# Triangular systems by block doubling: second products and subtraction over the changed columns alone, with constant matmuls ahead of them

## What is computed

```python
m = jnp.where(strict, jnp.einsum('nbhik,nbhjk->nbhij', k_beta, kc) * decay, 0.0)
a = jnp.eye(C, dtype=f32) + m
u = lax.linalg.triangular_solve(a, v_beta, left_side=True, lower=True, unit_diagonal=True)
w = lax.linalg.triangular_solve(a, k_beta * jnp.exp(gcum)[..., None],
                                left_side=True, lower=True, unit_diagonal=True)
```

## Time and profile before

| what | value |
|---|---|
| median of 3 executions | 2620.18 us (2619.04 to 2622.69) |
| the profiled execution | 2623.88 us, its span 2622.1 us |
| PE busy | 2503.3 us, 95% of the span |
| DVE busy | 1726.1 us, 66% |
| ACT busy, POOL busy | 1216.9 us, 657.5 us |
| stage of the triangular systems | 597.1 to 724.9 us of the span |

### The profile page before, as it was taken

One profiled execution on the slowest core, in us unless ns is written; L12 is line 12 of the kernel. 1 busy time (PEld: TensorE's weight loads), 2 busy tenths in 40 slices (PEclk: granted clock), 3 DMA queues, 4 the chain that ended last, 5 costly groups with the idle time before them and its releaser, 6 DMA issues.

```text
span 2622.1 us, 42984 instructions
## 1 busy us (share of the span) xinstructions
PE 2503.3 (95%) x16456; PEld 2171.4 (83%) x16456; DVE 1726.1 (66%) x3444; ACT 1216.9 (46%) x2307; POOL 657.5 (25%) x594
## 2 busy tenths in 40 slices
PE   8999999997879999999999999999999999999998
PEld 6777887886767877888888887789999889989998
DVE  4787487898776677356764456676663576746766
ACT  4322324751153523324433325656555568555684
POOL 0111112003213201112111122121135543655435
PEclk9999999998889999999999999999999999999999
DMA  7554452220002455333453442237544444444444
GB/s 285 170 183 161 144 177 81 81 89 2 2 1 72 162 181 173 136 132 125 157 177 133 156 145 76 97 105 249 190 158 151 138 153 140 167 145 145 154 137 145
DMA packets 119324, 359.05 MB, mean 137 GB/s; under 512 B 13136, under 2 KB 15312, under 8 KB 118736
## 3 DMA queue, kind: packets, MB, share of 16 engines
q1 hardware_dynamic: 119120, 356.30, 39.8%
HBM read 355.20 MB, written 1.05 MB: 136 GB/s over the span
## 4 chain that ended last, share of the span: by engine, by line
PE 72%; DVE 12%; ACT 6%; issue 4%; DMA 4%; POOL 2%; DVEq 0%; SPq 0%; POOLq 0%; ACTq 0%
PE ps L1954 20%; PE ps L1957 20%; PE ps L1955 19%; DMA ring<-w_stream 4%; ACT spl L2303 2%; DVE work L2573 2%; DVE big L2573 2%; DVE spl L2549 1%; PE ps L2018 1%; DVE big L2767 1%; PE ps L2211 1%; PE ps L1979 1%; PE ps L1981 1%; PE ps L1980 1%; PE ps L2248 1%
## 5 line engine op out<-in xcount | busy, mean ns | idle before, releaser
L1954 PE MATMUL ps<-bigr,spl 128*128 128x256 f32 (+1 forms) x3846 | 1307.4, 340 | 31.4 <-DVE spl L2549 24.3
L1957 PE MATMUL ps<-bigr,spl 128*128 128x256 f32 (+1 forms) x3846 | 1287.7, 335 | 3.5 <-POOL bigr L3030 3.2
L1955 PE MATMUL ps<-bigr,spl 128*128 128x256 f32 (+1 forms) x3846 | 1285.2, 334 | 0.0
L2549 DVE TENSOR_TENSOR spl<-ring,spl 128x512 fp32r<-128x512 f32 x838 | 657.9, 792 | 581.3 <-ACT spl L2303 578.1
L2303 ACT ACTIVATE spl<-ring 128x512 fp32r<-128x512 f32 x1024 | 629.9, 628 | 746.2 <-PE ps L1957 503.8
L1954 PEld LDWEIGHTS ps<-bigr,spl 128*128 128x128 f32 x3846 | 730.3, 190 | 129.9 <-DVE spl L2549 32.2
L1957 PEld LDWEIGHTS ps<-bigr,spl 128*128 128x128 f32 x3846 | 730.2, 190 | 84.1 <-POOL bigr L3030 10.3
L1955 PEld LDWEIGHTS ps<-bigr,spl 128*128 128x128 f32 x3846 | 730.8, 190 | 72.9 <-issue 1.7
L3030 POOL TENSOR_TENSOR bigr<-work,bigr 128x512 fp32r<-128x512 f32 (+1 forms) x192 | 198.5, 1037 | 925.0 <-ACT bigr L2307 924.9
L3025 POOL TENSOR_TENSOR spl<-ring,spl 128x512 fp32r<-128x512 f32 x186 | 253.8, 1365 | 275.0 <-ACT spl L2303 274.3
L2307 ACT ACTIVATE bigr<-work 128x512 fp32r<-128x512 f32 (+1 forms) x224 | 117.3, 526 | 259.8 <-DVE work L2633 163.0
(11 more groups left out here) (312 smaller groups left out, 2389.7 us busy)
## 6 DMA issues: line engine op xcount, KB each, us to landing
ring<-w_stream SPq DMA_DIRECT2D x512, 512.0 KB, 3.4
big<-w_stream SPq DMA_DIRECT2D x280, 256.0 KB, 3.1
big<-w_stream SPq DMA_DIRECT2D x16, 512.0 KB, 10.1
X<-x_t SPq DMA_DIRECT2D x2, 1024.0 KB, 15.4
cst<-consts SPq DMA_DIRECT2D x1, 1537.5 KB, 9.0
X<-mem_t SPq DMA_DIRECT2D x1, 1024.0 KB, 5.8
out_t<-X SPq DMA_DIRECT2D x8, 128.0 KB, 2.1
prm<-params SPq DMA_DIRECT2D x1, 252.5 KB, 2.7
```

Of the source, the lines that this page charges most:

```text
L1954: pe.matmul(out, hi, x[0], start=k == 0, stop=False)
L1955: pe.matmul(out, lo, x[0], start=False, stop=False)
L1957: finish(pe.matmul(out, hi, x[1], start=False, stop=k == nk - 1), tile, key if k == nk - 1 else None)
L2549: dve.tensor_tensor(lo_half(h), raw_half(h), hi_half(h), SUB).then_inc(*sig("lo", h, by="lo_dve"))
```

## The change

The tiles T and U of direction 1 change places (U comes first), and some of the tiles move to other columns, so that the changed columns of T and of U are one access pattern. `block_half` picks every second block of lv columns. The second products have 32 moving columns in place of 64 and write 32 columns each, packed, so that both products of a system fill 256 columns of the bank (128 at level 32). The subtraction goes over these alone. For direction 0, `level_u` on TensorE issues two matmuls on constants into the same bank, before it waits for the mask; the second products overwrite their result. The weights of all products stay 64x64 and their number stays as it was.

```diff
-        lane = [[(B(LN0 + d * 1024, 256), B(LN0 + d * 1024 + 256, 512), accQ[:, 0:256] if d else B(LN0 + 768, 256)) for d in range(2)],
-                [(w_[:, 0:256], arow[:, 512 * d:512 * d + 512], w_[:, 256:512]) for d, w_ in enumerate((w_mean, w_rstd))]]
+        def lane_of(d, whole, at, Mt, Pm):
+            first, second = whole[:, at:at + 256], whole[:, at + 256:at + 512]
+            T_, U_ = (second, first) if d else (first, second)
+            return Mt, T_, U_, Pm, whole[:, at:at + 576]
+
+        lane = [[lane_of(d, B(0, WK), LN0 + (1024 if d else 256), B(LN0 + (1536 if d else 0), 256), accQ[:, 0:256] if d else B(LN0 + 768, 256)) for d in range(2)],
+                [lane_of(0, arow, 0, w_rstd[:, 0:256], w_rstd[:, 256:512]),
+                 lane_of(1, work, 7 * 512, arow[:, 512:768], arow[:, 768:1024])]]
+
+        def block_half(ap, lv, x):
+            return ap.rearrange("p (n s i) -> p n s i", s=2, i=lv)[:, :, x, :]
+
+        def changed(d, lv, TU):
+
+            if lv == 32:
+                return block_half(TU[:, 0:256] if d else TU[:, 256:512], lv, 1 - d)
+            both = TU[:, 0:512 + 2 * lv].rearrange("p (u m) -> p u m", u=2)[:, :, 0:256]
+            return both.rearrange("p u (n s i) -> p u n s i", s=2, i=lv)[:, :, :, 0, :]
...
             def warm(n, bank, free):
                 w.all(free, done)
+                constants(bank, n)
+
+            def constants(bank, n):
                 w.wait_ge(*done("cond"))
                 moving = csr[:, 0:256].rearrange("p (o n) -> p o n", o=1).broadcast_to([128, 2, 256])
                 for _ in range(n):
...
             def level_u(h, d, lv, b, free):
-                _, TU, Pm = lane[h % 2][d]
-                w.all(free, done)
+                _, T_, U_, Pm, _ = lane[h % 2][d]
+                w.all(free, done)
+                if not d:
+                    constants(b, 2)
                 w.wait_ge(*done("lvp", h, d, lv))
+                to_t, to_u = (b[:, 128:256], b[:, 0:128]) if d or lv == 32 else (b[:, 0:128], b[:, 128:256])
                 for c in range(8):
                     p, t, rows = chunk(c)
                     cs_ = slice(t * 64, t * 64 + 64)
-                    us_ = slice(256 + t * 64, 256 + t * 64 + 64)
+                    at = slice(t * 32, t * 32 + 32)
                     if lv < 32:
-                        pe.matmul(b[rows, cs_], TU[rows, us_], Pm[rows, cs_], start=True, stop=True)
-                    ins = pe.matmul(b[rows, us_], Pm[rows, cs_], TU[rows, us_], start=True, stop=True)
+                        pe.matmul(to_t[rows, at], U_[rows, cs_], block_half(Pm[rows, cs_], lv, d), start=True, stop=True)
+                    ins = pe.matmul(to_u[rows, at], Pm[rows, cs_], block_half(U_[rows, cs_], lv, 1 - d), start=True, stop=True)
                 ins.then_inc(*sig("lvb", h, d, lv))
...
             def level_u(h, d, lv, b, free):
-                TU = lane[h % 2][d][1]
-                a = 0 if lv < 32 else 256
+                x = changed(d, lv, lane[h % 2][d][4])
+                if lv < 32:
+                    y = b[:, 0:256].rearrange("p (u n i) -> p u n i", u=2, i=lv)
+                else:
+                    y = b[:, 0:128].rearrange("p (n i) -> p n i", i=lv)
                 w.wait_ge(*done("lvb", h, d, lv))
-                dve.tensor_tensor(TU[:, a:512], TU[:, a:512], b[:, a:512], SUB).then_inc(*sig("tu", h, d, lv))
+                dve.tensor_tensor(x, x, y, SUB).then_inc(*sig("tu", h, d, lv))
```

More of the change, by code:

```diff
@@ L2092, in unit_turn @@
             def unit_turn(h, d, b, free):
-                U = lane[h % 2][d][1][:, 256:512]
+                U = lane[h % 2][d][2]
                 w.all(free, done)
@@ L2114, in level_p @@
             def level_p(h, d, lv, b, free):
-                Mt, TU, _ = lane[h % 2][d]
+                Mt, T_ = lane[h % 2][d][0:2]
                 w.all(free, done)
@@ L2121, in level_p @@
                     cs_ = slice(t * 64, t * 64 + 64)
-                    ins = pe.matmul(b[rows, cs_], Mt[rows, cs_], TU[rows, cs_], start=True, stop=True)
+                    ins = pe.matmul(b[rows, cs_], Mt[rows, cs_], T_[rows, cs_], start=True, stop=True)
                 ins.then_inc(*sig("lva", h, d, lv))
             def level_u(h, d, lv, b, free):
-                _, TU, Pm = lane[h % 2][d]
+                _, T_, U_, Pm, _ = lane[h % 2][d]
                 w.all(free, done)
+                if not d:
+                    constants(b, 2)
                 w.wait_ge(*done("lvp", h, d, lv))
+                to_t, to_u = (b[:, 128:256], b[:, 0:128]) if d or lv == 32 else (b[:, 0:128], b[:, 128:256])
                 for c in range(8):
@@ L2131, in level_u @@
                     cs_ = slice(t * 64, t * 64 + 64)
-                    us_ = slice(256 + t * 64, 256 + t * 64 + 64)
+                    at = slice(t * 32, t * 32 + 32)
                     if lv < 32:
-                        pe.matmul(b[rows, cs_], TU[rows, us_], Pm[rows, cs_], start=True, stop=True)
-                    ins = pe.matmul(b[rows, us_], Pm[rows, cs_], TU[rows, us_], start=True, stop=True)
+                        pe.matmul(to_t[rows, at], U_[rows, cs_], block_half(Pm[rows, cs_], lv, d), start=True, stop=True)
+                    ins = pe.matmul(to_u[rows, at], Pm[rows, cs_], block_half(U_[rows, cs_], lv, 1 - d), start=True, stop=True)
                 ins.then_inc(*sig("lvb", h, d, lv))
             def u_values(h, d, b, free):
-                Ub = lane[h % 2][d][1][:, 0:256]
+                Ub = lane[h % 2][d][1]
                 w.all(free, done)
@@ L2149, in w_keys @@
             def w_keys(h, d, bb, free):
-                Uw = lane[h % 2][d][2]
+                Uw = lane[h % 2][d][3]
                 w.all(free, done)
@@ L2412, in decay @@
             def decay(h, d, b, taken):
-                E = lane[h % 2][d][2]
+                E = lane[h % 2][d][3]
                 w.wait_ge(*done("de_min", h, d))
@@ L2418, in unit_turn @@
                 w.wait_ge(*done("ut", h, d))
-                act.activation(lane[h % 2][d][1][:, 0:256], b[:, 0:256], ACTF.Copy).then_inc(*sig("utc", h, d))
+                act.activation(lane[h % 2][d][1], b[:, 0:256], ACTF.Copy).then_inc(*sig("utc", h, d))
             def q_decay(h, d, b, free, e, efree):
@@ L2779, in decay @@
             def decay(h, d, b, taken):
-                Mt, _, E = lane[h % 2][d]
+                Mt, _, _, E, _ = lane[h % 2][d]
                 w.wait_ge(*done("grow", h, d))
@@ L2800, in level_p @@
             def level_p(h, d, lv, b, free):
-                Pm = lane[h % 2][d][2]
+                Pm = lane[h % 2][d][3]
                 w.wait_ge(*done("lva", h, d, lv))
@@ L2807, in level_u @@
             def level_u(h, d, lv, b, free):
-                TU = lane[h % 2][d][1]
-                a = 0 if lv < 32 else 256
+                x = changed(d, lv, lane[h % 2][d][4])
[3 more added lines that the diff above has]
+                    y = b[:, 0:128].rearrange("p (n i) -> p n i", i=lv)
                 w.wait_ge(*done("lvb", h, d, lv))
-                dve.tensor_tensor(TU[:, a:512], TU[:, a:512], b[:, a:512], SUB).then_inc(*sig("tu", h, d, lv))
+                dve.tensor_tensor(x, x, y, SUB).then_inc(*sig("tu", h, d, lv))
             def scale_u(h, d):
-                _, TU, Pm = lane[h % 2][d]
-                U = TU[:, 256:512]
+                _, T_, U, Pm, _ = lane[h % 2][d]
                 w.wait_ge(*done("tu", h, d, 32))
-                dve.tensor_tensor(four(TU[:, 0:256]), four(U), cA4[:, :, 2 + d, h:h + 1].broadcast_to([128, 4, 64]), MUL).then_inc(*sig("ub", h, d))
+                dve.tensor_tensor(four(T_), four(U), cA4[:, :, 2 + d, h:h + 1].broadcast_to([128, 4, 64]), MUL).then_inc(*sig("ub", h, d))
                 w.wait_ge(*done("cb"))
@@ L3056, in unit @@
             def unit(h, d, bG):
-                Mt, TU, _ = lane[h % 2][d]
-                U = TU[:, 256:512]
+                Mt, _, U = lane[h % 2][d][0:3]
                 w.wait_ge(*done("mm", h, d))
```

## The result

The changed kernel takes 2625.63 us in the median of 13 runs (2621.06 to 2632.17), the kernel before 2621.25 in the median of as many (2614.92 to 2623.85) beside it: a ratio of 1.002, 95% interval 1.0011 to 1.0028. So the change makes the kernel slower by 2 to 4 us. One of the 15 executions of the kernel before beside e10 to e13 took 2774.45 us at a mean clock of 0.844 against 0.984 to 0.987 in the others; it is left out, and the median of the other 14 is 2621.29.

The account below looks back on a forecast made before the run. No engine was taken to bound the stage alone; a chain changing between engines did. Subtractions -4.0, products 0, constants +5.3 and clock -2.6 gave -1.3 us, from 2620.18 to 2618.9 us; range 2607 to 2626 for 8 in 10.

Parts of the forecast that it names:

- Second products, priced at 0 on the path: TensorE's second products: halving moving columns saves nothing, since loading the weights sets the step of 30 ns; 0 us.
- 8-column row: Profile row: 128-column weights step at 110 ns with 8 moving columns, 111 ns with 128; taken as load setting the step.
- rival B: Second products do get cheaper, their step following the moving columns; -8.7 us in all, 2611.5 us; chance 0.20.
- rival D: Clock falls more often, behind pauses in three levels of heads 0 to 2; two falls of 3.5 us, +8.3 us; chance 0.14.
- Subtractions, -4.0 us: VectorE's subtractions on the chain get shorter: 0.27 us for each of eleven wide, 0.14 for each of seven level-32 ones.
- eleven wide and seven narrow pieces: Subtractions counted as lying on the chain of waits: eleven over 512 columns and seven of level 32; together 4.0 us.
- falls priced under the clock: Half-clock stretches from 652.4, 665.6 and 703.2 us, behind pauses before second products; priced at 3.0, 3.0 and 1.8 us.
- Constants, +5.3 us: Two constant matmuls ahead of direction 0's second products on TensorE, 0.48 us a time, delay those products at 11 places.
- eleven places: Of 20 constant pairs, those that push the second products: eight at 0.48 us, others at 0.3, 0.96 and 0.2.
- seven pauses: Places where TensorE waits 1.1 to 2.7 us for the mask, hiding the constants; without that cover they cost 3.4 us.
- Clock, -2.6 us: Constants in TensorE's pauses before second products make one of three clock falls go, at the mean price of 2.6 us.
- C: Rival: constants hold the clock at all three priced pauses before second products; -6.5 us, 2613.7 us; chance 0.16.

Follow-up runs that it names:

- e10: Second products read and write all 64 columns in stepped order, first blocks then second blocks, against e1; 2611.71 us, ratio to the kernel before 0.9960.
- e13: The kernel of e1 measured once more; 2611.43 us, ratio to the kernel before 0.9964.
- e1: Short subtractions alone, with whole second products and no constants, against the kernel before; 2612.87 us, ratio 0.9968.
- e3: Short subtractions and constants, but whole second products, against the kernel before; 2618.47 us, ratio 0.9993.
- e12: The changed kernel measured a second time; 2622.92 us, ratio to the kernel before 1.0009.
- e2: The changed kernel without its constant matmuls: short subtractions and half-width second products; 2624.20 us, ratio to the kernel before 1.0011.
- e9: e2 with the first products at half width too, so all 896 matmuls have 32 moving columns; 2637.83 us, ratio to the kernel before 1.0062.
- e6: e1 plus a constant pair only at the seven places where TensorE paused before direction 0's second products; 2613.08 us, ratio to the kernel before 0.9968.
- e5: The kernel before plus two constant matmuls ahead of direction 0's second products, nothing else; 2623.80 us, ratio 1.0010.
- e7: e1 with the first products at half width and the second ones whole; 2612.62 us, ratio to the kernel before 0.9965.

## Why the prediction was right and wrong

The forecast was -1.3 us and the sign was wrong. By the experiments the change is -8.8 us for the subtractions (before to e1), +5.6 for the constants (e1 to e3) and +7.2 for the thin products (e3 to changed), together +4.0. The forecast had -4.0, +5.3 less 2.6 for the clock, and 0. The step that failed is the pair of terms in which the clock stands: thin products at 0, and constants that win 2.6 us back with nothing lost elsewhere. Time at half clock did not go down, it went from 79 us to 92 (84 in e12). The subtractions were mis-sized by 4.8 us in the other direction. Without that the forecast would have missed by 10 us and not by 5, which is luck.

**Second products, priced at 0 on the path: right on the step, wrong on the cost.** The 8-column row led to the right duration, at both levels of the clock. The rival B (cheaper products) is excluded. But 0 was the price of the step alone. The change in the granted clock that thin products bring was left to rival D. Between e3 and the changed kernel, which differ in nothing else, it is 3.7 us of stage and 7.2 us of median (less, some 4.8, by the second measurement, each against the kernel before beside it). Without constants it is 11.3. This is the term that turned the sign.

**Subtractions, -4.0 us: mis-sized.** Their durations came as forecast, but alone they bring 8.8 and 9.9 us (e1, e13), and 11.0 of the stage (mean of the two). The reading of the chain was right: it does hold eleven wide and seven narrow pieces. What failed is that a piece was taken to give only its own length. At two places the taps that followed became shorter as well, by 2.4 us in all, and two of the falls priced under the clock went away without any constants, 3.0 and 1.8 us by my own prices. The sum of these, 4.0 + 2.4 + 4.8 = 11.2, is an estimate from the rows and meets the 11.0 of the stage. Another way to price the clock gives less. Between e1, e2 and e9 the stage grows by (125.4 - 114.1)/(55 - 18) = 0.3 us for each microsecond at half clock, and by 0.35 over the second step. The stages of e1 and e13 spend 9 to 12 us less at half clock than that of before, which by this is some 3 us. So the parts are shown, their shares only roughly.

**Constants, +5.3 us: near, for wrong parts.** With whole products and short subtractions they cost 5.6 us. A pair takes 0.7 us in place of 0.48, so eleven places at that price would be more than the 5.3. That at seven pauses they are hidden was right (e6).

**Subtractions and constants together.** Without the clock the sum had -4.0 + 5.3 = +1.3. Before to e3 it is -3.2 by the medians and -2.1 by stage, with 13 us less at half clock. The two do not add. Without constants the subtractions bring 8.8 us (11.0 of the stage), beside them 5.3 (e5 to e3; 2.4 of the stage, with 2 us more at half clock). One reason is in the traces: with constants and whole subtractions (e5) the way from subtraction to mask behind level 32 takes 3.0 and 3.2 us already, and in e3 3.1, so nothing is left to win there. My term for the subtractions was near the one that holds beside the constants.

**Clock, -2.6 us: the falls went, for another reason, and others grew.** Two of the three priced falls are gone in the changed kernel, one more than forecast. But with whole products they go by the short subtractions alone (e1), and the constants add little: half clock goes from 70 us to 67 (e3) and 66 (e6). Only beside whole subtractions do they take more, 11 us (before to e5). With thin products the two falls are back (e2), and there the constants do take them away. What the forecast lacked is the rest: the time at half level of the stage went up, from 30 us to 33 (38 in e12), through stretches that last longer.

**The rivals.** D named the right mechanism, that less streaming means less clock. Of its three places one has a fall now, head 0's level 4 (610.5 us, and again in e12); behind head 1's level 2 there is none, and at head 2's level 16 it comes 0.6 us after the start of the second products in e12, but only with the waits for GpSimd in the first execution, as before. Its price of a new fall, 3.5 us, was for a stretch of the usual length; what came was one of 17 us (13.7 in e12). That two falls of 3.5 are near the 7.2 us measured is luck. C had the constants holding the clock at all three places: with thin products they do at two. C's sum lacked what the thin products cost. B's sum is off in itself: -14.4 + 4 + 1.3 is -9.1 us, not -8.7.

The Trainium skill ("TensorE: Matmul & The Clock Gate", the part on the clock gate) says that throttled is the default and activity releases it. The runs agree, with the addition that activity is not what the busy records show (e9's window). The same page of the Trainium skill has a floor of about 25 ns under the step of narrow matmuls. It was not what bound here: the step is 29.5 ns at full clock and 54 at half, so what sets it slows with the clock, as the records of the loads do (135 and 223 ns in the changed kernel too).

## What to carry to other kernels

Halving the moving side of these matmuls saved nothing on TensorE, whose step stayed at 29.5 ns, and cost granted clock. Look first for a row with fewer moving columns and the same weights, and ask of a thinner TensorE load what it does to the clock. Take the shorter PSUM reads on VectorE and leave the products whole, writing the surplus columns where nobody reads them. When a change has several parts, price each alone: here one part won 9 us and the other two lost 13. And when an instruction on the chain gets shorter, look at what starts behind it: here it was worth more than the instruction itself.

## What the runs showed that was not expected

- TensorE busy in 23.96 of 24 us at a mean clock of 0.52 (e9, all products with 32 moving columns); the same count of instructions with 64 moving columns ran the whole stage at 0.92.
- The first products alone at half width changed nothing (e7, 2612.62 us against 2612.87), one direction of the second products did (e8), and spread its runs over 19 us. The reason is open.
- A tap of VectorE takes 0.75 us or 1.78 us according to whether it starts 0.1 us before a GpSimd multiply or 0.03 us after it; the multiply then takes 1.77 or 1.27.
- The same pause of 1.1 us in front of second products is followed by a fall of the clock where they are thin (e2) and by none where they are whole (e1).
- Patterns that step over blocks of 2 to 32 elements cost nothing that could be measured, neither in VectorE's subtraction from PSUM (0.41 us for 256 columns, as contiguous) nor in TensorE's moving side and output (e10).
- A microsecond of this stage at half clock goes with 0.3 to 0.35 us more of the stage, not 0.5 (an estimate from the profiled executions of e1, e2 and e9).
